# The low part of each weight unit on GpSimd: two operations of 512 columns in place of one of 1024

## The reference

```python
def swiglu_ffn(x, w_gu, w_down):            # first block
    gu = x @ w_gu
    g, u = gu[..., :FFN_HIDDEN], gu[..., FFN_HIDDEN:]
    return (jax.nn.silu(g) * u) @ w_down

def conv_ffn(h, w_up, cw, cb, w_down):      # second block
    u = dwconv3(h @ w_up, cw) + cb
    g, val = jnp.split(u, 2, axis=-1)
    return (jax.nn.silu(g) * val) @ w_down

def second_block(x, c, ctx, ...):
    for l in range(DEPTH):
        ...                                  # mixer on x and ctx
        x = x + g2 * conv_ffn(h2, ffn_up[l], ffn_conv_w[l], ffn_conv_b[l], ffn_down[l])
        if not last:
            ...
            ctx = ctx + cg2 * conv_ffn(h2c, ffn_up[l], ffn_conv_w[l], ffn_conv_b[l], ffn_down[l])
    return x
```

## Time and profile before

| | us |
|---|---|
| median of 3 runs | 2835.73 (2831.59 to 2838.17) |
| the profiled execution | 2834.38 |
| its span in the trace | 2832.6 |
| PE busy, share of the span | 2766.6, 98% |
| PEld busy | 2591.4, 91% |
| POOL busy | 1950.2, 69% |
| ACT busy | 1406.2, 50% |
| DVE busy | 1061.2, 37% |
| mean granted clock of PE | 0.982 of full |

### The profile page before, as it was taken

The page is one execution under the profiler, slowest core; times in us unless marked ns, Lnnn a source line. Parts: engine busy times, 40 slices in busy tenths (PEclk is TensorE's granted clock), DMA queues, the critical chain, the costliest instruction groups (busy, mean ns, idle before and its releaser), DMA issues.

```text
span 2832.6 us, 51824 instructions
## 1 busy us (share of the span) xinstructions
PE 2766.6 (98%) x21902; PEld 2591.4 (91%) x21902; DVE 1061.2 (37%) x2065; ACT 1406.2 (50%) x1939; POOL 1950.2 (69%) x816
## 2 busy tenths in 40 slices
PE   7999989999999899999999999999999999999999
PEld 6899879999899799998999998888999988889999
DVE  3333331123323232242544334445434344543434
ACT  4656434445664434445554444555544445564443
POOL 6557638866568348867676887775667877657687
PEclk9999989999999989999999999999999999999999
DMA  7446455565556445555444555643445555435453
GB/s 265 164 179 223 141 187 186 180 216 186 186 188 220 150 169 182 185 209 176 150 155 149 173 185 168 208 164 130 139 149 186 180 198 178 140 128 171 142 184 129
DMA packets 136520, 495.76 MB, mean 175 GB/s; under 512 B 15073, under 2 KB 17377, under 8 KB 135137
## 3 DMA queue, kind: packets, MB, share of 16 engines
q1 hardware_dynamic: 131904, 480.53, 49.6%
q10 hardware_dynamic: 4384, 11.93, 1.2%
HBM read 489.26 MB, written 3.15 MB: 174 GB/s over the span
## 4 chain that ended last, share of the span: by engine, by line
PE 91%; DVE 3%; ACT 3%; DVEq 1%; issue 1%; ACTq 0%; POOL 0%; DMA 0%; SPq 0%
PE lin L520 18%; PE lin L521 17%; PE lin L522 17%; PE aux L520 5%; PE aux L522 5%; PE aux L521 5%; PE lin L546 4%; PE lin L548 4%; PE lin L547 4%; PE aux L615 2%; PE aux L968 1%; PE aux L986 1%; PE aux L696 1%; PE lin L661 1%; PE aux L661 1%
## 5 line engine op out<-in xcount | busy, mean ns | idle before, releaser
L496 POOL TENSOR_TENSOR wlo<-raw,whi 128x1024 fp32r<-128x1024 f32 x812 | 1950.0, 2419 | 873.1 <-ACT whi L1076 872.0
L1076 ACT ACTIVATE whi<-raw 128x1024 fp32r<-128x1024 f32 x812 | 845.3, 1057 | 752.7 <-PE lin L522 553.5
L520 PE MATMUL lin<-in_hi,whi 128*128 128x256 f32 x3520 | 1013.2, 288 | 27.2 <-POOL wlo L496 23.2
L521 PE MATMUL lin<-in_lo,whi 128*128 128x256 f32 x3520 | 998.7, 284 | 0.0
L522 PE MATMUL lin<-in_hi,wlo 128*128 128x256 f32 x3520 | 998.4, 284 | 0.0
L520 PEld LDWEIGHTS lin<-in_hi,whi 128*128 128x128 f32 x3520 | 677.9, 193 | 61.7 <-issue 56.8
L521 PEld LDWEIGHTS lin<-in_lo,whi 128*128 128x128 f32 x3520 | 678.2, 193 | 0.7
L522 PEld LDWEIGHTS lin<-in_hi,wlo 128*128 128x128 f32 x3520 | 677.9, 193 | 0.0
L520 PE MATMUL aux<-br_hi,whi 128*128 128x256 f32 x880 | 249.2, 283 | 0.0
L521 PE MATMUL aux<-br_lo,whi 128*128 128x256 f32 x880 | 249.0, 283 | 0.0
L522 PE MATMUL aux<-br_hi,wlo 128*128 128x256 f32 x880 | 249.0, 283 | 0.0
(11 more groups left out here) (246 smaller groups left out, 3543.7 us busy)
## 6 DMA issues: line engine op xcount, KB each, us to landing
raw<-in_wstream SPq DMA_DIRECT2D x908, 512.0 KB, 3.3
Z<-in_rel ACTq DMA_DIRECT2D x2, 1536.0 KB, 8.9
Z<-in_mem_t ACTq DMA_DIRECT2D x2, 1024.0 KB, 5.5
kv_store<-Z ACTq DMA_DIRECT2D x2, 1024.0 KB, 6.9
Z<-kv_store ACTq DMA_DIRECT2D x2, 1024.0 KB, 14.4
x<-in_x_t SPq DMA_DIRECT2D x1, 1024.0 KB, 5.0
Z<-in_ctx_t SPq DMA_DIRECT2D x1, 1024.0 KB, 4.8
out_x<-x SPq DMA_DIRECT2D x1, 1024.0 KB, 3.9
```

The source lines that it names most:

```text
L496: pool.tensor_tensor(wlo[s][:, :], raw[i % RAWS][:, :], whi[s][:, :].bitcast(F32), ALU.subtract).then_inc(lo_pool, 1)
L520: pe.matmul(out, wh, xh, start=start, stop=False, skip_group_check=True)
L521: pe.matmul(out, wh, xl, start=False, stop=False, skip_group_check=True)
L1076: act.activation(whi[s % SLOTS][:, :], raw[i % RAWS][:, :], ACT.Copy).then_inc(hi_ready, 1)
```

## The change

For each divided unit POOL issues two `tensor_tensor` operations in place of one: the first on columns 0 to 511, the second on columns 512 to 1023 (`CH` is 512). Both compute the same difference as before. The wait for `hi_ready` stands ahead of the first, and the count of `lo_pool` goes up with the second alone. So no other engine sees a unit sooner than when both are done. POOL has 1624 such operations in place of 812.

```diff
                     s = order[i] % SLOTS
                     pool.wait_ge(hi_ready, order[i] + 1)
-                    pool.tensor_tensor(wlo[s][:, :], raw[i % RAWS][:, :], whi[s][:, :].bitcast(F32), ALU.subtract).then_inc(lo_pool, 1)
+                    for h in range(2):
+                        w = slice(h * CH, (h + 1) * CH)
+                        part = pool.tensor_tensor(wlo[s][:, w], raw[i % RAWS][:, w], whi[s][:, w].bitcast(F32), ALU.subtract)
+                    part.then_inc(lo_pool, 1)
```

## The result

The changed kernel takes 2848.9 us (median of 14 runs, 2834.0 to 2850.4) where the kernel before took 2838.2 in the same comparison (14 runs, 2829.7 to 2845.1): a ratio of 1.0027, 95% interval 1.0015 to 1.0039. It is slower, by some 11 us by the medians and some 8 by the ratio, where the prediction had it faster by 7. A second comparison gave 2846.0 us against 2838.3, 1.0024 [1.0009, 1.0039].

What follows compares the result with a forecast made beforehand. PE was taken as the bound, so only its idle and low-clock time could move. Gains of 9.6 us less 2.3 us for the fixed time gave 7.3 us faster, 2828.4 us by the median; range 2823 to 2845.

Steps and rivals of the forecast that it cites:

- PE is the bound, POOL has room: Whole kernel: PE 98% busy, POOL 69% and waiting for ACT's copy, so more POOL work is free in the mean.
- Gains at the start, the forget gates, the merged branches and the attention norms: Shorter DVE waits for POOL cut PE's idle time: 0.5, 2.3, 2.3 and 2.2 us.
- Gain at the gating: Gating values, L2177: two DVE waits of one POOL operation each are cut; gain 2.25 us, all of PE's idle time there.
- The rival in which POOL keeps its turn between the halves: DVE waits as long as before and only the 2.3 us cost stays: 2838.0 us; chance 0.1.
- The fixed time a: Extra fixed time of one more POOL operation per unit, taken as 0.12 us; cost 19a = 2.3 us.
- the bounds: Limits for a: 0.033 us from POOL's memsets below, 0.21 us from ACT's two widths above.
- DVE's pair: Middle case: a of 0.14 to 0.18, 0.16 by DVE's two widths; net 2.7 us faster, 2833.0 us; chance 0.2.
- 23 steps: Steady feed-forward steps of the second block: each loses 6a - 0.79 us, nothing up to a = 0.13.
- 19 x 0.142: The 19a cost: eight units PE waits for (8a) plus the last steps of three feed-forward parts (11a); forecast 2.3 us.
- The rival of the multiply that meets POOL's burst: Feed-forward steps: a longer POOL burst delays DVE's multiply; at a = 0.21, net 5.9 us slower, 2841.6 us; chance 0.2.
- the eight units: Units, besides that of 30.77, for which PE stands and waits, as at 346; cost 8 x a.
- The lower clock: Behind the 3.63 us idle PE runs 6.6 us at clock 0.50; avoiding it would add 3.3 us gain, to 2823.4.

Runs made afterwards that it cites:

- wait in 24 units: Changed kernel, but in the eight units around each of three gatings POOL's second half waits for the first; 2830.0 us, ratio 0.9970 to the kernel before.
- whole in the feed-forward: Halves with that wait at 24 gating units, but whole operations in 3 x 66 units of the long feed-forward stretches; 2827.8 us, ratio 0.9963 to before.
- three pauses: Changed kernel, but only in units 330, 504 and 662 the second half waits for the first; 2829.4 us, ratio 0.9971 to the kernel before.
- the small kernels: Network left out, input copied to output; POOL runs with DVE operations asking at varied points, varied widths and traffic. They time the port; no total time given.
- quarters: Each unit's low part in four POOL operations of 256 columns in place of the changed kernel's two of 512; 2930.0 us (one run).

## Why the prediction was wrong, step by step

- *PE is the bound, POOL has room*: right. POOL went from 69 to 73%.
- *Gains at the start, the forget gates, the merged branches and the attention norms, 7.3 us*: right in each place that can be read. 1.06 of the 1.15 us forecast at each forget gate (3.63 to 2.57), 0.96 at the merged branches (1.39 to 0.43), the rest gone.
- *Gain at the gating, 2.25 us*: wrong, and this is the step that failed. It rested on the sentence "DVE gets its turn at every boundary, though POOL's next operation has all it waits for", read from the earlier trace rows. The rows show it, but for the first four operations of a run and for the 9th and 10th; no row of before has DVE asking later in a run than that. The change halves the operations and so doubles their number between two pauses: at the second gating 9 became 16, across a limit at 11 to 14. At the third it was 1 and became 17, since the pauses of 0.32 us between POOL's units there closed as well, which the prediction didn't look at. In place of a gain of 2.25 there is a cost of about 12 us at two gatings. At the first (1257.98 us) POOL had paused just before, and the pair was let in.
- *The rival in which POOL keeps its turn between the halves* named the right mechanism, a turn that POOL doesn't give up, and bounded it wrongly. It put it inside a unit, where there is no semaphore, and held that DVE would then wait as long as before, 2838.0. It lies at all boundaries late in a run, and its price is not one operation but the rest of the run.
- *The fixed time a = 0.12 us*: it is 0.142. POOL's run of twelve takes 15.08 us where that of six took 14.23, 0.85 more or 0.142 a unit:

```profile
1600.20 15.08 POOL L498 TENSOR_TENSOR wlo<-raw,whi 128x512 fp32r<-128x512 f32 x12 [2.24 <-ACT whi L1079]
...
1614.99 0.83 DVE L1542 TENSOR_TENSOR Z<-Z 128x512 f32<-128x512 f32 x1 [0.75 <-ACT Z L1336]
```

  It lies between the bounds, on the side of DVE's pair (0.16). The multiply meets the burst by 0.14 us (0.83 in place of 0.69), and the step grows by 6 x 0.142 - 0.79 = 0.06; measured nothing in the first steps of a stretch and 0.05 in the late ones. That is 1 us in 23 steps. With 19 x 0.142 = 2.7 the cost of a comes to 3.7 us in place of 2.3. The rival of the multiply that meets POOL's burst is thus right in its mechanism and small at this a. The Trainium skill's 4497 ns for 2048 columns (GPSIMD Engine Reference, Reconciling with measured numbers), from which an estimate of 0.24 was worked out, does not agree with the 0.142 measured here.
- *What is left of the sum*: 9.6 - 3.7 = 5.9 us without stands. It can be read as idle time of PE, span less busy, which the clock touches little. Before 66.0 and 65.9 us in two profiles; without stands 60.2 (wait in 24 units), 59.9 (in 3) and 60.1 (whole in the feed-forward), so 5.8 to 6.1 less; with the two stands 72.6 and 70.0. That 5.9 meets 5.8 to 6.1 is in part luck: the 1 us of the 23 steps does not stand in the idle time, since PE is busy for 17.30 of 17.30 us, while the waits of PE at the eight units grew by 2.3 us together in the changed kernel, where 8a gives 1.1. By the medians the kernels without stands are 8.3 and 10.5 us below before.
- *The lower clock*: the prediction had it only as a possible gain. PE's busy time, the same matmuls in all, is 2775.7 and 2775.6 us in the kernels with both stands, 2764.2 in that with three pauses and 2766.6 and 2769.7 in before, but also 2774.6 in one without any stand. Some 10 to 13 us of the 15 to 17 between with and without are idle time; the rest is clock. Only the two windows behind the stands are seen to follow from them, and how the clock falls elsewhere stays open.

The Trainium skill (SBUF — State Buffer, SBUF: two separate sides) says of the shared ports that the one who starts first has the lock and the other is blocked until it ends. This fits DVE's waits of one operation, 1.2 us here, and says nothing of who is next; the 8.10 us of one 128x512 operation are seven such turns in a row.

## What to carry to other kernels

Work cut into smaller pieces on POOL shortens each wait of DVE for the shared port, but the number of pieces that follow each other without a pause counts too: here, beyond 11 to 14, DVE was shut out in most cases, and then nearly always until POOL paused. Before cutting, count POOL's operations from its last pause to the time at which DVE asks on the critical path, after the cut, and look whether short pauses between its units will still be there; where the count comes near ten, make POOL wait once for its own last operation, which costs 0.1 us. And a rule read off rows ("is let in at every boundary") holds for the range of those rows alone: write down that range beside it, and look whether the change leaves it.

## What the runs showed of the hardware

- DVE is let in at the next boundary between two POOL operations that follow each other closely, as long as POOL has started about ten or fewer since it paused (29 of 29 pairs in the small kernels); from the 15th on it was passed over in 31 of 32, for the rest of the run, up to 29.9 us. The limit in these kernels goes with the number of operations: about the same for 256, 512 and 1024 columns, for `tensor_scalar` and `tensor_tensor`, with and without traffic of PE, ACT and DMA. The large kernels have exceptions: the operation on 48 columns let in at the 18th, and with quarters stands that ended within a run, as that of 13.2 us, after 19 boundaries.
- A pause of 0.08 us, one wait of POOL for its own operation, sets it back. DVE operations of 128x64 let in after every second unit kept DVE from being shut out (12 of 12, at most five operations behind one); a turn of 128x1 nine operations earlier did not.
- A POOL subtraction has 0.142 us of its own beside its columns, from two halves against one whole beside the other engines' work.
- What it is in the chip that counts, the traces don't tell. The records of neighbouring POOL operations overlap, by 0.03 us in some stands and by 0.12 in the first one of the changed kernel's second profile, and by 0.03 to 0.08 where DVE was let in; so the overlap is not the sign of it.
